# Hybrid DeltaNet and windowed attention layer on one Trainium2 core: three small products and one attention step of TensorE set in one row

## What is computed

```
h = x @ w_in                                   # all projections
# group A, per head and chunk of tokens
a_mat = where(strict, (k*beta) @ k.T * decay, 0)
t_mat = inverse(eye + a_mat)                   # unit lower triangular
v_new = t_mat @ (v*beta) - (t_mat @ (k*beta*exp(g))) @ s
o     = (q*exp(g)) @ s + (where(causal, q @ k.T * decay, 0)) @ v_new
s     = s * gt + k_dec.T @ v_new
# group B, per pair of heads and block of 128 queries over 256 keys
p = exp(score*scale - slope*dist - m); p = p / (sum(p) + exp(sink - m)); o = p @ v
y = concat(rms_norm(oA)*silu(zA), oB*silu(zB)) @ w_out
out = layer_norm(alpha*x + y)
```

## Time and profile before

| what | value |
|---|---|
| runs | 1092.45, 1095.0, 1096.09 us |
| median | 1095.0 us |
| profiled execution: span | 1092.9 us; the page gives no other time for it |
| TensorE busy | 1066.5 us, 98% of the span |
| VectorE busy | 688.6 us, 63% |
| ScalarE busy | 532.4 us, 49% |
| GpSimd busy | 115.7 us, 11% |
| mean granted TensorE clock | 0.996 of full speed |

### The profile page before, as it was taken

How to read it: one execution, slowest core, us unless ns; L and a number is a source line. 1 busy time by engine, 2 the same in 40 slices (tenths; PEclk the granted TensorE clock), 3 DMA queues, 4 the chain that set the end, 5 groups by cost and what they waited for, 6 DMA issues and landing times. The chain is left out here.

```text
span 1092.9 us, 19513 instructions
## 1 busy us (share of the span) xinstructions
PE 1066.5 (98%) x7212; PEld 848.9 (78%) x7212; DVE 688.6 (63%) x2081; ACT 532.4 (49%) x1557; POOL 115.7 (11%) x152
## 2 busy tenths in 40 slices
PE   7999999999999999999999999999999999999997
PEld 5877787778778787787887878787787878787885
DVE  5286959585654748667365674757637575758565
ACT  4556675754635444373263645436344655464300
POOL 3513132134100000011000000002000000002210
PEclk9999999999999999999999999999999999999999
DMA  8967475665552717253463461715355343522432
GB/s 276 313 214 261 160 276 194 243 205 180 188 194 105 251 64 237 70 204 114 159 197 139 126 242 50 258 62 184 107 183 176 126 157 127 207 77 66 136 116 77
DMA packets 58430, 183.55 MB, mean 168 GB/s; under 512 B 8480, under 2 KB 21216, under 8 KB 45024
## 3 DMA queue, kind: packets, MB, share of 16 engines
q1 hardware_dynamic: 58192, 182.05, 49.0%
q10 hardware_dynamic: 144, 0.26, 0.1%
HBM read 138.22 MB, written 44.07 MB: 167 GB/s over the span
## 5 line engine op out<-in xcount | busy, mean ns | idle before, releaser
L847 PE MATMUL bank<-xr,w 128*128 128x512 f32 x2496 | 656.7, 406 | 10.9 <-DVE xr L1532 7.7
L847 PEld LDWEIGHTS bank<-xr,w 128*128 128x128 f32 x2496 | 451.7, 190 | 105.9 <-issue 13.6
L898 PE MATMUL bank<-wo,y_split 128*128 128x512 f32 x432 | 114.5, 404 | 0.0
L898 PEld LDWEIGHTS bank<-wo,y_split 128*128 128x128 f32 x432 | 77.1, 189 | 14.5 <-issue 0.7
L1580 DVE SCALAR_TENSOR_TENSOR kq<-conv_in,convw_all,kq 128x512 f32<-128x512 f32 x96 | 77.2, 805 | 8.2 <-ACT conv_in L1189 6.2
L1485 ACT ACTIVATE o_scaled<-bank 128x128 f32<-128x128 f32 x64 | 17.7, 276 | 123.7 <-PE bank L1119 123.5
L1351 ACT ACTIVATE score<-score,neg_max 128x256 f32<-128x256 f32 (+1 forms) x128 | 62.7, 493 | 29.2 <-DVE neg_max L1757 29.2
L1917 DVE TENSOR_SCALAR steps<-bank,nb_rk 128x128 f32<-128x128 f32 x64 | 22.3, 348 | 63.9 <-PE bank L1115 63.9
L1920 DVE SCALAR_TENSOR_TENSOR state<-state,cols_all,bank 128x128 f32<-128x128 f32 x64 | 22.2, 347 | 63.2 <-PE bank L1118 63.2
L1791 DVE TENSOR_TENSOR y_step<-blocks,y_cols 128x60 f32<-128x60 f32 (+14 forms) x240 | 50.1, 209 | 9.7 <-DMA blocks<-n_spill 1.0
L781 POOL TENSOR_TENSOR xr<-y_tile,xr 128x256 fp32r<-128x256 f32 x8 | 5.9, 773 | 460.1 <-ACT xr L1170 460.1
(11 more groups left out here) (217 smaller groups left out, 1628.8 us busy)
## 6 DMA issues: line engine op xcount, KB each, us to landing
w<-w_split SPq DMA_DIRECT2D x78, 1024.0 KB, 5.7
w_split<-w SPq DMA_DIRECT2D x26, 1024.0 KB, 5.1
blocks<-n_spill SPq DMA_DIRECT2D x32, 256.0 KB
y_spill<-y_out SPq DMA_DIRECT2D x30, 256.0 KB, 5.8
x_tile<-w_in SPq DMA_DIRECT2D x13, 512.0 KB, 5.9
y_tile<-w_in SPq DMA_DIRECT2D x12, 512.0 KB, 6.5
y_tile<-y_spill SPq DMA_DIRECT2D x12, 512.0 KB, 6.1
x_tile<-x SPq DMA_DIRECT2D x12, 512.0 KB, 3.9
```

The lines of the kernel that those rows point to most:

```text
L847: ins = nc.tensor.matmul(bank[JOBS[at].bank][:], w[:, turn % 3, wp, k, :], xr[:, xp, k], start=(step == 0), stop=(step == 3 * KT - 1))
L898: ins = nc.tensor.matmul(bank[JOBS[at].bank][:], y_place(t)[:, yp, k], wo[:, k, wp, half * UNIT:(half + 1) * UNIT], start=(step == 0), sto ...
```

## The change

In the work of TensorE the fill places between P1 and P3 are taken out. P1, the scores of the second half, P2, the values of the first half (before: ahead of P1) and P3 stand in one row with no filler between. The row is placed at 0.6 of a level behind the old place of P1; P4 is 0.4 of a level earlier than it was, P5 and the turns of the second half too. VectorE's and ScalarE's orders follow.

```diff
-        self.p16, self.y16, self.p32, self.y32, self.p64 = (first + level * a for a in range(5))
+        self.p16, self.y16, self.y32, self.p64 = (first + level * a for a in (0.6, 1.6, 2.6, 3.6))
...
                 fill_to(n, at.p16)
-                values(n, 0)
                 after(pe, t_ready, n, 1)
                 after(pe, pt_ready, n, 2)
                 quads_of(lambda c, rows: nc.tensor.matmul(quad_place(bank[6], rows, c), n_t[rows, c, rows], t0[rows, c],
                                                           start=True, stop=True)).then_inc(inv_done.sem, 1)
                 scores(n, 1)
-                fill_to(n, at.y16)
                 after(pe, r_ready, n, 1)
                 after(pe, v_tok_ready, n, CH)
                 quads_of(lambda c, rows: nc.tensor.matmul(quad_place(bank[4], rows, c), r16[rows, c], y0[rows, c],
                                                           start=True, stop=True)).then_inc(inv_done.sem, 1)
-                fill_to(n, at.p32)
+                values(n, 0)
                 after(pe, t_ready, n, 2)
...
                 nc.scalar.activation(y16, quad_tiles(bank[4]), ACT.Copy).then_inc(inv_copied.sem, 1)
-                weights(n, 1, (0,))
-                after_jobs(n, at.y16)
                 take(p32, quad_tiles(bank[6]), 3)
-                weights(n, 1, (1,))
+                weights(n, 1)
+                after_jobs(n, at.y16)
...
+                after(dve, inv_done, n, 2)
+                nc.vector.transpose(t16, quad_tiles(bank[4])).then_inc(t_ready.sem, 1)
                 gate_b(n, 0)
+                after(dve, t_ready, n, 2)
+                for b in range(2):
+                    rows = slice(b * QUAD, (b + 1) * QUAD)
+                    nc.vector.tensor_copy(t32[rows, :, rows], t16[rows])
+                maxima(n, 1)
                 if t is not None and i < AH - 1:
                     split_y(t)
                 else:
                     convs(n, 0.34, 1)
-                maxima(n, 1)
-                after(dve, inv_done, n, 2)
-                nc.vector.transpose(t16, quad_tiles(bank[4])).then_inc(t_ready.sem, 1)
-                after(dve, t_ready, n, 2)
-                for b in range(2):
-                    rows = slice(b * QUAD, (b + 1) * QUAD)
-                    nc.vector.tensor_copy(t32[rows, :, rows], t16[rows])
...
-                after_jobs(n, at.p32)
+                after_jobs(n, at.y16)
```

More of the change, by code:

```diff
@@ L1444, in slot @@
                 nc.scalar.activation(y16, quad_tiles(bank[4]), ACT.Copy).then_inc(inv_copied.sem, 1)
-                weights(n, 1, (0,))
+                take(p32, quad_tiles(bank[6]), 3)
+                weights(n, 1)
                 after_jobs(n, at.y16)
-                take(p32, quad_tiles(bank[6]), 3)
-                weights(n, 1, (1,))
                 after(act, inv_copied, n, 1)
@@ L1903, in slot @@
                     split_y(11)
-                convs(n, at.p32)
+                convs(n, at.y16)
                 after_jobs(n, at.step0)
```

## The result

The changed kernel takes 1110.06 us (median of 4 runs, 1107.94 to 1114.88), the kernel before took 1095.55 us in the same comparison (4 runs, 1092.45 to 1099.17). The ratio is 1.0156, with a 95% interval of 1.0131 to 1.0181. The direction was the forecast one, but the size was not: 14.5 us instead of 6.4, and outside the range of 1093 to 1106.

The account below looks back on a forecast made before the run. TensorE, busy 98% of the span, bounds the kernel; other engines' waits count only where it stands still. Slot terms 6.4 - 0.3 - 1.8 - 0.1 + 1.5 + 1.1 - 0.4 = +6.4 us on 1095.0 give 1101.4; range 1093 to 1106.

Parts of the forecast that it names:

- What TensorE saves: Between first turns and P4, four filler runs become two, each costing 0.22 us: 0.44 us a slot, 7.0 in 16 slots.
- lower end: On TensorE, new neighbours or the mode-change count leave only half the saving: 0.22 us a slot, 3.5 in all.
- rival (c): New neighbourhoods on TensorE cost a full price, halving the saving in eleven slots: +2.4 us, 1103.8; chance 0.12.
- Slots 0 to 2: Late gating delays P5's transpose; TensorE waits 2.2 us, turns come at 11.88: +2.15 us a slot, +6.4 in three.
- rival (b): Longer waits lower TensorE's clock; in slots 0 to 2, 3 x 1.7 = 5 us more, 1106.5; chance 0.10.
- Slots 6 and 10: VectorE's chain, including an output tile's addition, ends as before, so TensorE waits what it saves: -0.1 us.
- Slots 7 and 11: Two layer norm operations delay the copy for P2, which waits 1.3 us: 0.75 us a slot, +1.5 in all.
- Slots 12 to 14: In these short slots the turns wait 0.7 to 0.8 us for VectorE's division: +0.36 us a slot, +1.1 in all.
- Slot 15: Last slot keeps TensorE's saving, taken as in slot 4: -0.4 us.
- Slot 3: No weight for VectorE, so it keeps the saving less 0.12 us more wait at P1: -0.3 us.
- Slot 4: With slots 5, 8 and 9: division ends before the turns need it, no wait; 4 x 0.44 = -1.8 us.
- rival (d): Slot 4's wait for a weight tile goes; up to 4.6 us (2.9 and 1.7) come back, 1096.8; chance 0.06.

Follow-up runs that it names:

- experiment 5: Changed kernel with VectorE's order remade for the new row (output tile's half and weight ahead of P3's transpose, layer norm at old place): 1086.69 us, ratio to before 0.9945.
- experiment 1: Changed kernel with the output tile's low part (split_y) on VectorE moved ahead of P3's transpose: 1105.39 us, ratio to the kernel before 1.0122.
- experiment 2: Changed kernel with the weight's low part (slots 0 to 2) on VectorE moved ahead of P3's transpose: 1109.53 us, ratio to the kernel before 1.0158.
- experiment 4: Changed kernel with VectorE's due work ahead of P2, the layer norm in slots 7 and 11, at its old place: 1110.38 us, ratio to before 1.0167.
- experiment 6: Kernel of experiment 5 with three or four fillers moved ahead of the turns in slots 12 to 15, layer norms later: 1085.06 us, ratio to before 0.9928.
- experiment 11: Kernel of experiment 5 run again unchanged, as a repetition: 1087.71 us, ratio to the kernel before 0.9959.
- experiment 3: Changed kernel with the last two convs ahead of P5's transpose put behind the division (slots 0 to 2): 1107.94 us, ratio to the kernel before 1.0134.

## Why the prediction was right or wrong

**What TensorE saves: right, with a lower end that was too low.** 0.44 us a slot was forecast from two run prices of 0.22. Slots 5, 8 and 9 lost 0.47, 0.47 and 0.49, and one run added by itself costs 0.24 to 0.26. So rival (c), in which half of it goes, falls. The rule of the Trainium skill (TensorEngine Tiling (Array Packing), Key Properties), that a change of tiling mode drains TensorE, was weighed beside this with two changes saved a slot (eight, then six), at half a run price each, 0.22 in all. The runs agree with the count and not with my price of one: two changes fewer gave 0.47, one more (scores to fillers to P2, for scores to P2) cost 0.24 to 0.26. Counting runs and counting changes with some 0.24 for each fit all of it equally, and no run here parts the two. What the rows add is that the small products leave in the same time whoever comes next: the scores pass to P2 in 130.25 - 129.18 = 1.07 us in experiment 5 and to fillers in 131.58 - 130.51 = 1.07 before; P2 passes to the values in 0.38, P3 to fillers in 0.37. The 0.22 lies inside the run of fillers, about half at each end, as the prediction said (entering and leaving). Three narrow windows of the kernel before show it, on the run ahead of P2 (P2 starts at 132.93):

```profile
131.58 0.50 PE L847 MATMUL bank<-xr,w 128*128 128x512 f32 x1
...
131.91 1.09 PE L847 MATMUL bank<-xr,w 128*128 128x512 f32 x4
...
132.62 0.39 PE L847 MATMUL bank<-xr,w 128*128 128x512 f32 x1
```

From the first filler to the second 0.33 us pass, from the second to the fifth (0.71 us) 0.24 each, from the fifth to P2 0.31. The part at the end is missing ahead of the turns, which are full 128x128 products: there five fillers take 137.92 - 136.65 = 1.27 us (experiment 5), not 1.35.

**Slots 0 to 2: mechanism and places right, size short by the clock.** Gating 2.75 behind P1, P5 at 9.40 (9.37 forecast), waits of 0.76 for the weight and 1.12 for the transpose (2.2 forecast for both). The turns were forecast at 11.88 and came at 12.69, since the granted clock fell to 1.2 GHz behind the waits, in each of the three slots. This is rival (b), given a chance of 0.10, with the price at 1.7 a slot; it is 0.9 here (+3.06 against +2.15 a slot; 0.94 in experiment 1). Slot 0 of experiment 1 has the same waits at the full clock, and there the turns come at 11.84, so the forecast's path is right and the clock is all that it lacks. The argument against it, that other waits of about one us did not do it, took them one at a time, where here two stood within 3 us; in experiment 2 one wait of 1.5 was followed by a drop in two slots. Experiment 5 shows the cause by removing it: with VectorE's order repaired the gating is as late, the waits are gone, and so is the low clock.

**Slots 6 and 10: wrong, the largest miss.** The step that failed is "VectorE's chain ends at the same time as before, so what TensorE saves it waits. -0.1". It followed the chain to its end and looked only at who waits there. But the diff also moves `split_y` from ahead of the maxima to behind gating, copies and maxima, and its reader, the first matmul of the output projection, comes in the middle of the chain. The parts stood in the prediction itself: values from 1.83 with 1.02 for eight put P3 at 2.85 behind P1, and L1757, the maxima's end, at 5.25 (measured 5.26); only `split_y` and its reader were not set against them. In the changed kernel L898 is due at 442.68 + 0.97 - 439.45 = 4.2; L1717 starts at 444.99 - 439.45 = 5.54 and ends at 6.76. The wait was 2.71 in both slots, plus the clock in slot 6: +5.7 where -0.1 was forecast. Experiment 1 moved that one operation and took 3.55 and 2.04 us out of the two slots, back to what the forecast had said.

**Slots 7 and 11: right**, +0.86 and +0.66 for 0.75: P2 waits 1.2 behind the layer norm (1.3 forecast). That the lengths agree to 0.1 is partly luck, since slot 7 alone is 78.90 and 77.98 in two executions of one program. Taking it away showed no gain in experiment 4: P2's waits went, but in that execution the x tile came late in these slots.

**Slots 12 to 14: right in the path, the sum with luck.** The turns come 9.44 behind P1 for 9.35 forecast and wait 0.61 to 0.64 for 0.7 to 0.8. (By the prediction's own terms the division ends at 7.65 + 0.4 + 1.14 = 9.19, not 9.25.) The sum is +1.2 for 1.1, but it is made of 0.04, 0.38 and 0.79 where 0.36 each was forecast, and slot 12 of one program differs by 1.5 between two executions. **Slot 15: wrong**, +1.1 for -0.4; it was taken "as in slot 4" without a look at its own rows. L1113 waits 1.4 there, the turns 0.7. **Slot 3: wrong by 0.7**; the turns wait 0.42 for a sum of VectorE (L1591), which no step named. The other 0.3 isn't accounted for, and slot 3 of one program differs by 0.6 between two executions.

**Slot 4: rival (d) in part.** The wait for the weight tile shrank from 2.9 to 0.9 and no low clock followed it, and the wait at L955 grew from 0.3 to 1.0: -3.5 where -0.4 was forecast. With -2.1 for the wait, +0.7 for L955 and -0.5 for the row, some 1.6 are left for the clock, an estimate. Experiments 5, 6 and 11, which are one program up to there, have slot 4 at 66.72, 62.70 and 63.33, so slot 4's length moves by some 4 us with no change of the program, and most of its gain here may be luck. It hid 3 us of the loss: without it the forecast would have been wrong by more.

The misses add up: 5.8 (slots 6, 10) + 2.8 (clock) + 1.5 (slot 15) + 0.7 (slot 3) - 3.1 (slot 4) = 7.7, the difference between +14.2 and +6.5.

**What the change is worth.** With a VectorE order of its own TensorE's new row is 0.55% faster than the kernel before (0.9945, and 0.9959 in the repetition), and the same care for VectorE without the new row gives nothing (0.9988). So the idea was sound: 16 x 0.47 = 7.5 us on TensorE, of which 4.7 to 5.7 arrive. The loss of 1.56% is the VectorE order that came with it. Open is why the clock fell in some places and not in others after the same wait (slot 10 for slot 6; slot 0 for slot 1 in experiment 1), why it cost 0.9 us in one place and 1.5 in another, and when the x tile's transfer is late.

## What to carry to other kernels

When an instruction moves, list every operation that its engine's queue now holds behind it, with the reader and the due time of each, and not only the end of the chain: the largest loss here was one VectorE operation of 1.2 us, whose inputs were ready, queued behind a gating that had become late. Work that waits for nothing belongs into the gap in which the queue waits anyway; in slots 1, 6 and 10 of experiment 5 it cost nothing there. It must truly wait for nothing: in slot 4 the output tile's low part had to wait for ScalarE and held P3 up for 1.34 us. And where several waits of about one us gather within a few us, price the lower clock that can follow them as well.

## What the runs showed of the hardware

- The same waits did and did not bring TensorE's clock down: 0.75 and 1.11 us in slot 0 of experiment 1, with no drop, 0.75 and 1.12 in slot 1, with one; 2.71 us in slots 6 and 10 of the changed kernel, with a drop in the first alone, and the same 2.71 in experiments 3 and 4, with a drop in both. A stretch at 1.2 GHz lasted 3.4 us and cost 0.9 to 1.6 us: 0.94 in experiment 1, 67.04 - 65.53 = 1.5 between slots 6 and 10, and 54.07 - 52.16 = 1.9 between slots 1 and 2 of experiment 2, of which 0.3 is the shorter wait at P5.
- Some operations of VectorE are slower beside GpSimd: in slot 1 of the changed kernel two convs of L1577 take 1.88 us together, for 1.53 in experiment 5 at a place where GpSimd does nothing, and the division's four operations 1.82 us where they took 1.14 in slot 6, while GpSimd worked on its part of the weight in slot 1 and did nothing in slot 6. The maxima, which read a bank, were not: 0.42 us each in slot 1 of experiment 5 beside GpSimd, 0.42 in slot 1 of the changed kernel without it.
- The transfer of an x tile in slot 7 landed 6.4 us after its issue in the changed kernel and 9.3 in experiment 4, and 7.9 and 6.3 in experiments 5 and 11, which are the same program. In experiment 4 TensorE waited 2.0 us behind it.
